# Feed-forward with seven products: the sums of inputs and weights made by VectorE instead of GpSimd, the ordinary tiles squared by ScalarE

## The reference, cut to what matters

```python
# second block
m = rmsnorm(h, g_mlp[i])
h = h + jnp.square(jax.nn.relu(m @ w_up[i])) @ w_down[i]
# third block
h = rmsnorm_3(x, norm_mlp_g[l])
x = x + jnp.square(jax.nn.relu(h @ w_mlp1[l])) @ w_mlp2[l]
```

## Time and profile before

| | |
|---|---|
| median of 3 runs | 4710.16 us (4697.45 to 4712.71) |
| profiled execution | 4700.76 us, its span 4699.0 us |
| PE busy | 4270.1 us, 91% |
| DVE busy | 2091.5 us, 45% |
| ACT busy | 1603.2 us, 34% |
| POOL busy | 636.8 us, 14% |
| feed-forward of block 2 | from 2629 us; its down stage from 2962.6 us |
| feed-forward of block 3 | from 3981 us; its down stage from 4316.4 us |

### The profile page before, as it was taken

How to read it: one execution, slowest core, us unless ns; L and a number is a source line. 1 busy time by engine, 2 the same in 40 slices (tenths; PEclk the granted TensorE clock), 3 DMA queues, 4 the chain that set the end, 5 groups by cost and what they waited for, 6 DMA issues and landing times. The chain is left out here.

```text
span 4699.0 us, 67316 instructions
## 1 busy us (share of the span) xinstructions
PE 4270.1 (91%) x28429; PEld 3475.5 (74%) x28429; DVE 2091.5 (45%) x2868; ACT 1603.2 (34%) x2680; POOL 636.8 (14%) x508
## 2 busy tenths in 40 slices
PE   7988899987979979899998899999989878999998
PEld 5988889756958858677434688888767676788887
DVE  4544425363345552324443466433442363666333
ACT  3732235242243332311575433222332333433221
POOL 0024400010001100002231332000100001321001
PEclk8989999998989999999999999999999898999999
DMA  3110012122110021111000133421111221234222
GB/s 112 38 60 2 2 41 70 49 65 81 45 36 9 9 78 45 62 42 45 32 10 27 56 115 108 148 95 59 53 33 41 57 47 45 94 112 153 82 94 72
DMA packets 323010, 284.91 MB, mean 61 GB/s; under 512 B 19569, under 2 KB 288145, under 8 KB 322594
## 3 DMA queue, kind: packets, MB, share of 16 engines
q1 hardware_dynamic: 322722, 280.76, 19.3%
HBM read 204.55 MB, written 55.31 MB: 55 GB/s over the span
## 5 line engine op out<-in xcount | busy, mean ns | idle before, releaser
L3116 PE MATMUL ff_acc<-ff_x_hi_rounded,ff_wh_rounded 128*128 128x512 f32 x1024 | 399.8, 390 | 5.2 <-DVE ff_x_rounded L3335 5.2
L3116 PE MATMUL ff_acc<-ff_x_rounded,ff_wh_rounded 128*128 128x512 f32 x1024 | 399.2, 390 | 0.0
L3116 PE MATMUL ff_acc<-ff_x_hi_rounded,ff_wl_rounded 128*128 128x512 f32 x1024 | 399.2, 390 | 0.0
L3095 PE MATMUL ff_bank<-ff_x_hi_rounded,ff_wh_rounded 128*128 128x512 f32 x784 | 308.8, 394 | 17.0 <-issue 9.6
L3095 PE MATMUL ff_bank<-ff_x_hi_rounded,ff_wl_rounded 128*128 128x512 f32 x784 | 308.0, 393 | 0.0
L3095 PE MATMUL ff_bank<-ff_x_rounded,ff_wh_rounded 128*128 128x512 f32 x784 | 308.0, 393 | 0.0
L3116 PEld LDWEIGHTS ff_acc<-ff_x_hi_rounded,ff_wh_rounded 128*128 128x128 f32 x1024 | 192.7, 188 | 46.8 <-DVE ff_x_rounded L3335 6.9
L3184 ACT ACTIVATE ff_wh_rounded<-ff_wl 128x512 fp32r<-128x512 f32 x128 | 80.6, 632 | 417.2 <-DMA ff_wl<-w_mlp_dram 207.7
L3116 PEld LDWEIGHTS ff_acc<-ff_x_hi_rounded,ff_wl_rounded 128*128 128x128 f32 x1024 | 192.7, 188 | 39.9
L3116 PEld LDWEIGHTS ff_acc<-ff_x_rounded,ff_wh_rounded 128*128 128x128 f32 x1024 | 192.6, 188 | 39.9
L3405 DVE TENSOR_TENSOR all_hid<-all_hid,ff_acc 128x1024 f32<-128x1024 f32 x64 | 78.2, 1221 | 303.0 <-PE ff_acc L3116 303.0
(11 more groups left out here) (642 smaller groups left out, 10628.6 us busy)
## 6 DMA issues: line engine op xcount, KB each, us to landing
inner<-ff_made_out SPq DMA_DIRECT2D x64, 512.0 KB, 2.6
ff_x<-inner SPq DMA_DIRECT2D x64, 512.0 KB, 5.6
ff_wl<-w_down_dram SPq DMA_DIRECT2D x64, 256.0 KB, 3.1
ff_wl<-w_mlp_dram SPq DMA_DIRECT2D x64, 256.0 KB, 3.0
ff_raw<-w_up_dram SPq DMA_DIRECT2D x30, 512.0 KB, 4.2
ff_raw<-w_mlp_dram SPq DMA_DIRECT2D x30, 512.0 KB, 4.3
mid_w<-w_in_dram SPq DMA_DIRECT2D x104, 128.0 KB, 2.7
pa_w<-w_in_dram SPq DMA_DIRECT2D x72, 128.0 KB, 2.7
```

The source lines that it names most:

```text
L3095: mm = M(to, rounded(a[:, j, h, :]), rounded(b[:, j, h, :]), start=(j in (0, 1, 5) and h == 0 and i == 0), stop=(h == H - 1 and i == 2), s ...
L3116: mm = M(acc[:, s, c, :], rounded(a[:, s, k, :]), rounded(b[:, at, c * W2:(c + 1) * W2]), start=(k == 0 and i == 0), stop=(k == KD - 1 and ...
```

## The change

- Inputs: `scale_x` keeps one instruction for each h (blocks 2 and 3 of `x_hi`). The sums are made by VectorE straight from `hid`: 16 scalar_tensor_tensor instructions of 128x512 (`sum_x`: `hid` times gain, less a block made before), four for each of block 4, `t3`, block 2 and block 3. `high_t` waits for all 16. The order of the blocks is now 4, 2, 3, 1 (before 4, 2, 1, 3), and TensorE's waits follow.
- Weights: `combine` moves to VectorE as two pieces of two instructions, put behind low(q+1, 0) and low(q+1, 1). The first piece waits for both halves of `raw`.
- GpSimd keeps only the sums of squares at the end.
- Ordinary tiles: ScalarE reads them with Relu and squares them in place by a second instruction; VectorE only multiplies by the row (`weigh_plain`).
- The queues of the start are reordered: the first two `high_x` and the first `low_x` go ahead of the first weights, the explicit load of the activation table at the head is gone, `high(2, 0)` and `low(2, 0)` go behind three splits of the input sums, the split of `t3` goes behind `copy(1, 0)` and high(2, 2).
- At the crossing to the down stage y 6 and 7 are split before w 1 and before the last read-out and shape.

```diff
@@ -3088,7 +3088,7 @@
                 if j == 6:
                     pe.wait_ge(dve_read, dve_reads(q) + 2)
                 if q == PLAIN and j in (1, 2, 3, 4):
-                    pe.wait_ge(t_low, {4: 1, 2: 2, 1: 3, 3: 4}[j])
@@ -3122,8 +3122,6 @@
         @block.scalar
         def _(act):
             A = nc.scalar.activation
-            nc.scalar.preload_act_table_set("natural_log_exp_and_others")
@@ -3149,22 +3147,18 @@
 
             def scale_x(h):
                 A(x_hi[:, 2:4, h, :], cut(hid[:, h, :]), ACT.Copy, scale=gain[:, h:h + 1]).then_inc(scaled, 1)
-                lower, g = cut(hid[:, h + H, :]), gain[:, h + H:h + H + 1]
-                A(x_hi[:, 4, h, :], lower[:, 1, :], ACT.Copy, scale=g).then_inc(scaled, 1)
-                A(x[:, 3, h, :], lower[:, 0, :], ACT.Copy, scale=g).then_inc(scaled, 1)
 
             def high_t(t, j, what):
                 if j == 1:
-                    act.wait_ge(summed_x, 1)
                     act.wait_ge(product, products(1) + 3)
-                else:
-                    act.wait_ge(third, 2 * H if j != 3 else 2 * H + 1)
-                    act.wait_ge(summed_x, 1)
+                act.wait_ge(summed_x, 4 * H)
                 A(rounded(x_hi[:, j]), what, ACT.Copy).then_inc(t_high, 1)
 
             def copy(q, i):
                 act.wait_ge(product, products(q) + 2 * (i + 1))
-                A(cut(made_out[:, q % 2, i, :]), plain_acc[q, i], ACT.Copy).then_inc(act_read, 1)
+                A(cut(made_out[:, q % 2, i, :]), plain_acc[q, i], ACT.Relu).then_inc(act_read, 1)
+                act.wait_ge(act_read, act_reads(q) + i + 1)
+                A(made_out[:, q % 2, i, :], made_out[:, q % 2, i, :], ACT.Square).then_inc(shaped, 1)
@@ -3183,29 +3177,33 @@
                     act.wait_ge(w_in[s][a], 16 * (m // 2 + 1))
                     A(rounded(w_hi[:, s, a * H:(a + 1) * H, :]), w[:, s, a * H:(a + 1) * H, :], ACT.Copy).then_inc(d_high, 1)
 
-            for u in range(2):
-                high_plain(0, u)
-                for h in range(H):
-                    high_x(u * H + h)
+            high_x(0)
+            high_x(1)
+            high_plain(0, 0)
+            for k in range(2, H):
+                high_x(k)
+            high_plain(0, 1)
+            for k in range(H, KD):
+                high_x(k)
             high_plain(0, 2)
             high_plain(0, 3)
+            for h in range(H):
+                scale_x(h)
             scale.root(act)
             copy(0, 0)
-            for h in range(H):
-                scale_x(h)
             high_plain(1, 0)
             high_plain(1, 1)
             copy(0, 1)
             high_plain(1, 2)
             high_plain(1, 3)
-            copy(1, 0)
-            high(PLAIN, 0)
             high_t(0, 4, x[:, 4])
             high_t(1, 2, x[:, 2])
+            high_t(2, 3, x[:, 3])
+            high(PLAIN, 0)
+            copy(1, 0)
             high(PLAIN, 1)
-            high_t(2, 1, t3)
-            high_t(3, 3, x[:, 3])
             high(PLAIN, 2)
+            high_t(3, 1, t3)
             copy(1, 1)
             for j in range(3, J):
                 high(PLAIN, j)
@@ -3219,12 +3217,10 @@
             high_y(0)
             high_y(1)
             high_w(0)
-            for i in range(2, 6):
+            for i in range(2, KD):
                 high_y(i)
             high_w(1)
             read(LAST, 6)
-            high_y(6)
-            high_y(7)
 
@@ -3249,33 +3245,6 @@
         def _(pool):
...
-            def combine(q):
-                pool.wait_ge(raw_in[0], 16 * q)
-                if q > PLAIN:
-                    pool.wait_ge(product, products(q - 1) + 2)
-                T(wl[:, 1], a11, a21, ALU.subtract).then_inc(combined, 1)
-                pool.wait_ge(raw_in[1], 16 * q)
-                pool.wait_ge(combined, sums_made(q) + 1)
-                T(a21, a21, a22, ALU.add).then_inc(combined, 1)
-                if q > PLAIN:
-                    pool.wait_ge(product, products(q - 1) + 3)
-                pool.wait_ge(combined, sums_made(q) + 2)
-                T(wl[:, 2], a21, a11, ALU.subtract).then_inc(combined, 1)
-                if q > PLAIN:
-                    pool.wait_ge(w_low, products(q))
-                pool.wait_ge(combined, sums_made(q) + 3)
-                T(fourth[:, :, :], a12, wl[:, 2], ALU.subtract).then_inc(combined, 1)
-
-            for h in range(H):
-                pool.wait_ge(scaled, 3 * h + 2)
-                T(x[:, 4, h, :], x_hi[:, 3, h, :], x_hi[:, 2, h, :], ALU.subtract).then_inc(third, 1)
-                pool.wait_ge(third, 2 * h + 1)
-                T(x[:, 2, h, :], x_hi[:, 4, h, :], x[:, 4, h, :], ALU.subtract).then_inc(third, 1)
-            pool.wait_ge(scaled, 3 * H)
-            pool.wait_ge(third, 2 * H)
-            T(x[:, 3], x[:, 3], x[:, 2], ALU.subtract).then_inc(third, 1)
-            for q in range(PLAIN, PAIRS):
@@ -3292,6 +3261,24 @@
                 dve.wait_ge(w_high, products(q) + u + 1)
...
+            def combine(q, j):
+                if j == 1:
+                    for a in range(2):
+                        dve.wait_ge(raw_in[a], 16 * q)
+                    if q > PLAIN:
+                        dve.wait_ge(product, products(q - 1) + 2)
+                    T(wl[:, 1], a11, a21, ALU.subtract).then_inc(combined, 1)
+                    dve.wait_ge(combined, sums_made(q) + 1)
+                    T(a21, a21, a22, ALU.add).then_inc(combined, 1)
+                else:
+                    if q > PLAIN:
+                        dve.wait_ge(product, products(q - 1) + 3)
+                        dve.wait_ge(w_low, products(q))
+                    dve.wait_ge(combined, sums_made(q) + 2)
+                    T(wl[:, 2], a21, a11, ALU.subtract).then_inc(combined, 1)
+                    dve.wait_ge(combined, sums_made(q) + 3)
+                    T(fourth[:, :, :], a12, wl[:, 2], ALU.subtract).then_inc(combined, 1)
+
             def low(q, j):
                 dve.wait_ge(w_high, products(q) + j + 1)
                 if j == 2:
@@ -3304,10 +3291,11 @@
                 V.scalar_tensor_tensor(rounded(x[:, at, k % H, :]), cut(hid[:, k, :]), gain[:, k:k + 1], rounded(x_hi[:, at, k % H, :]),
                                        ALU.mult, ALU.subtract).then_inc(x_low, 1)
 
+            def sum_x(to, k, c, less):
+                V.scalar_tensor_tensor(to, hid[:, k, c * W2:(c + 1) * W2], gain[:, k:k + 1], less, ALU.mult, ALU.subtract).then_inc(summed_x, 1)
+
             def low_t(t, j, what):
                 dve.wait_ge(t_high, t + 1)
-                if j == 2:
-                    dve.wait_ge(third, 2 * H + 1)
                 T(rounded(x[:, j]), what, rounded(x_hi[:, j]), ALU.subtract).then_inc(t_low, 1)
@@ -3316,18 +3304,19 @@
                 to, what = {3: (part_of(q, 1, 0), Y), 4: (part_of(q, 1, 1), X(q)), 5: (part_of(q, 0, 0), Z)}[j]
                 T(to, to, what, ALU.add).then_inc(dve_read, 1)
 
+            def weigh_plain(q, i):
+                dve.wait_ge(shaped, 2 * q + i + 1)
+                if q == 0:
+                    dve.wait_ge(scale.rooted, 1)
+                T(made_out[:, q % 2, i, :], made_out[:, q % 2, i, :], row, ALU.mult).then_inc(made, 1)
+
             def shape(q, i):
-                if q < PLAIN:
-                    dve.wait_ge(act_read, act_reads(q) + i + 1)
-                else:
-                    dve.wait_ge(dve_read, dve_reads(q) + 3 - i)
-                    if i == 0:
-                        dve.wait_ge(act_read, act_reads(q) + 4)
+                dve.wait_ge(dve_read, dve_reads(q) + 3 - i)
+                if i == 0:
+                    dve.wait_ge(act_read, act_reads(q) + 4)
                 a = made_out[:, q % 2, i, :]
                 V.scalar_tensor_tensor(a, a, 0.0, a, ALU.max, ALU.mult).then_inc(shaped, 1)
-                dve.wait_ge(shaped, 2 * q + (1 if i == first_half(q) else 2))
-                if q == 0:
-                    dve.wait_ge(scale.rooted, 1)
+                dve.wait_ge(shaped, 2 * q + 2 - i)
@@ -3341,34 +3330,50 @@
                     dve.wait_ge(d_high, 2 * m + a + 1)
                     T(rounded(w[:, s, part, :]), w[:, s, part, :], rounded(w_hi[:, s, part, :]), ALU.subtract).then_inc(d_low, 1)
 
-            for u in range(2):
-                low_plain(0, u)
-                for h in range(H):
-                    low_x(u * H + h)
+            low_x(0)
+            low_plain(0, 0)
+            for k in range(1, H):
+                low_x(k)
+            low_plain(0, 1)
+            for k in range(H, KD):
+                low_x(k)
             low_plain(0, 2)
             low_plain(0, 3)
-            shape(0, 0)
+            for h in range(H):
+                dve.wait_ge(scaled, h + 1)
+                sum_x(x[:, 4, h, :], h, 1, x_hi[:, 2, h, :])
+            for h in range(H):
+                sum_x(t3[:, h, :], h + H, 1, x_hi[:, 3, h, :])
+            weigh_plain(0, 0)
+            for h in range(H):
+                dve.wait_ge(summed_x, h + 1)
```

(33 more changed lines are left out.)

1 line of the change is left out of this document (removed).

## The result

| | before | after |
|---|---|---|
| median of 5 runs | 4710.16 us (4696.03 to 4712.74) | 4669.08 us (4666.91 to 4676.59) |
| ratio after / before | | 0.9928, 95% interval 0.9909 to 0.9946 |
| profiled execution, its span | 4700.76, 4699.0 us | 4676.59, 4674.8 us |
| up stretch of block 2 / block 3 | 333.46 / 335.59 us | 318.99 / 319.39 us |
| last stretch (down stage of block 3 to the end) | 382.64 us | 378.35 us |

A forecast was written before the change was run, and what follows sets the result against it. TensorE sets the pace, with time to win where it idles: A 2.4 + B, C 5.2 + D 11.1 + E 7.8 + F 7.2 = 33.7 us, 4667.1 profiled, 4676.5 as median. Range 4660 to 4695, the forecast's own 4672 to 4684.

The forecast's parts named there:

- A: Start of each part: first ordinary product waits 2.25 us for the first input tile's low part; gain 2.4 us.
- B: Before pair 1: a wait of 1.1 us for low parts of weights goes; 5.2 us together with C.
- C: Middle of pair 1: a wait of 1.2 us for low parts of weights goes; 5.2 us together with B.
- D: Pair 2, product 1: the wait for the split of an input sum goes; gain 11.1 us.
- E: Pair 2, product 3: the wait for read(2, 1), behind a weight transfer, shrinks to 2.4 us idle; gain 7.8 us.
- F: First tile of the down stage: the wait for low_y(6) goes; gain 7.2 us.
- The weight sums in the pairs: Four more VectorE instructions of 0.6 us a pair cost 0, covered by TensorE's 19 us.
- rival 3: Weight sums close a loop from load to next load in the pairs: slower, 4725 us; chance 0.04.
- Rival 1: Early work ends late and E keeps its size: 19.7 us gained, 4690.5 us; chance 0.20.
- Rival 2: Sums on VectorE keep D and E; only B, C and F go: 12.4 us, 4697.8 us; chance 0.08.

The follow-up runs named there:

- Experiment 3: The changed kernel with weight sums, input sums or squares, then both kinds of sums, back on their old engines: up stretches 318.92 to 320.67 us.
- experiment 6: The changed kernel with six idle 128x512 VectorE instructions added in every seven-product pair: median 4693.33 us, ratio to the kernel before 0.9977.
- experiment 2: The changed kernel's queue order with every sum and square back on its old engine: ratio to the kernel before 0.9953.
- experiment 1: The changed kernel with the crossing's order undone: last stretch 381.33 us; the kernel before with only the new crossing order: 378.21 us.

## Why the prediction was right, step by step

Forecast 4676.5 us, a gain of 33.7; measured 4669.08 and, by the ratio, 33.9. The places and their causes were right; one term, A, was sized wrong, and that the total agrees so closely is partly luck, as the sum below shows. Its terms, against the two traces:

- **A**, forecast 2.4, measured about 6.3: the size failed. The start came 1.74 and 1.86 us earlier (1.56 reckoned). But I then took some of it back for a clock that would rise at the old moment. It rose sooner, 4.0 us after the first ordinary product in block 2 and 1.8 in block 3, against 5.95: 0.8 and 1.9 us more. In the ten microseconds from that product the granted clock was 0.79; before it was 0.70, in the row below. TensorE had stood idle 0.5 us ahead of it in place of 2.25. How soon it rises is not fixed by the code: in the 22 parts of eleven traces with this head the slow matmuls at the start cost 0.15 to 2.4 us, 0.85 in the mean, in the four parts with the old head (before, and the crossing alone) 1.4 to 2.8, 2.4 in the mean. So about 1.6 us a part can be expected again, not each single value.

```profile
2635.00:2645.00 10.00, 9.82 (x31) 7.88 (x32) 10.00 (x11) 9.52 (x11) 0.00 (x0) 0.70 0.01 2
```

- **B, C**, forecast 5.2: both gaps gone. low_plain(1, 0) was done at 2664.05, wanted 96 matmuls after 2644.23 at 2667.95: 3.9 us in hand (forecast 4.4). low_plain(1, 2) and (1, 3) were done by 2672.17, wanted at 2678.8. Experiment 3 brings B back with GpSimd's sums, C never.
- **D**, forecast 11.1: gone with its slow matmuls. The load of pair 2 was issued 32.2 us after L225, before 44.8. The split of t3 ended at 2688.96, wanted 204 matmuls after the start at 2692.4: 3.5 us in hand (forecast 3.2).
- **E**, forecast 7.8, measured 3.7 + 3.7 = 7.4. The gap of 2.36 and 2.38 us was forecast as 2.4; the chain had the load issued 5.2 us after the last ordinary product, and it was (ScalarE's copy at 2689.97 to the issue at 2695.18). The slow matmuls behind it, taken as 0.8, were 0.1 and 1.7.
- **F**, forecast 7.2: the down stage of block 2 with what follows up to the next part's first weights shortened from 363.9 to 360.8 us (3326.57 less 2962.63, 3319.75 less 2958.95), 3.1 (0.3 of it in the wait at its end, 2.82 and 2.54 us in the rows), and the last stretch by 4.3: 7.4. The rows of PE, before and then after:

```profile
2962.63 0.39 PE L3116 MATMUL ff_acc<-ff_x_hi_rounded,ff_wh_rounded 128*128 128x512 f32 x1
...
3326.57 0.47 PE L2810 MATMUL ple_acc<-ple_m_hi_rounded,ple_w_hi_rounded 128*128 128x512 f32 x1 [2.82 <-DVE ple_m_rounded L2889]
```

```profile
3319.75 0.47 PE L2810 MATMUL ple_acc<-ple_m_hi_rounded,ple_w_hi_rounded 128*128 128x512 f32 x1 [2.54 <-DVE ple_m_rounded L2889]
```

- **The weight sums in the pairs**, forecast 0: no wait of PE, 215 of 215 us. The cover I named, TensorE's 19 us against VectorE's busy time with 7 free, was the wrong measure; rival 3's closed loop is the right one, and experiment 6 shows it.

With B, C and D at their forecast prices the sum is 37.4 us, against 14.5 + 16.2 + 7.4 = 38.1 in the stretches; 3.1 us of it were lost again in untouched code between the parts, a stretch that scatters by some 4 us between the traces, which leaves 35.0, and the head took back 10.8 in the profiled executions (4699.0 - 4674.8 = 24.2), though not in the ratio. So the 33.9 of the ratio come 0.2 from the forecast because a term 3.9 too small and 3.1 us lost elsewhere offset each other, and its interval (25 to 43) is far wider than the difference. The time of 4676.5 also took over the 9.4 us between the median and the profiled execution of before; after, the median lies 7.5 below the profiled one. The measured 4669.08 is therefore under the narrow range that the prediction gave its forecast (4672 to 4684) and inside the wide one (4660 to 4695).

Rival 1 (E keeps its size) fell: the transfer took 4.0 us. Rival 2 (only B, C, F go) fell; experiment 2 shows that even the old engines would have given more than its 12.4 us. Rival 3 did not happen, but its mechanism is real.

What I had not separated is why D and B went. The prediction named VectorE's relief (5.62 for 1.23 us) and the new order side by side. By experiments 2 and 3 the order carries 56 and 69% of the up stretches' gain in these executions (each stretch good to some 2 us), and the rest needs the squares and the sums not to meet on VectorE beside GpSimd.

## What to carry to other kernels

When a tuned kernel's bounding engine idles only at stage changes, list each idle time with what stands ahead of its releaser in that engine's queue: six gaps reckoned so gave 33.7 us, of the 38.1 that the stretches won. Reorder queues first and move work between engines second, and test the moves together: single ones can look free while two are not. Work added to a half-idle engine is free only up to the loop that it lies in (load, use, release, next load), which in experiment 6 was full with VectorE busy for 87% of the time.

## What the runs showed of the hardware

- VectorE instructions with two inputs were slowed beside GpSimd sums: of four of 128x512 the one that ran beside a GpSimd sum of 4.90 us took 5.12 us, the one ahead of it 1.77, the two behind it 0.68 each.
- The price of a TensorE gap of 2.4 to 2.6 us varied between 0.1 and 3.0 us of matmuls at half clock behind it: in experiment 1 these two values stand behind gaps of 2.63 and 2.62 us, with the same code, in two parts of one execution.
- A table load at the head of a part, where ScalarE had been idle, took 1.28 us and put TensorE's start 0.5 and 0.6 us off; no further time of it shows.
- The time of untouched code ahead of the parts scattered by 11 us (2628.9 to 2640.3) between executions, more than most of the single edits here are worth.
